# A hybrid decoder layer: the first adaLN sums in quarters of 256 channels, slots turned one pair ahead, one wait fewer before the router's sigmoid

## What is computed

```python
c_act = silu(c)
mod = c_act @ ada_w + ada_b                   # 1024 x 6144: shift, scale, gate of the mixer, then of the MoE
u = rms_norm(x) * norm_mix_g * (1 + scale_a) + shift_a
proj = u @ w_in                               # 1024 x 10760: q, k, v, o, gates of mLSTM; q, k, v of attention; g_m, g_a
y = sigmoid(g_m) * (mlstm(...) @ w_branch_m) + sigmoid(g_a) * (attention(...) @ w_branch_a)
x = x + gate_a * (y @ w_out)
v = rms_norm(x) * norm_ffn_g * (1 + scale_f) + shift_f
scores = sigmoid(v @ router_w)                # group-limited top 2 of 16 experts
x = x + gate_f * sum_e combine[e] * (silu(v @ w_gate[e]) * (v @ w_up[e])) @ w_down[e]
out = rms_norm(x) * final_norm_g
```

## Time and profile before

| what | value |
|---|---|
| median of three runs | 605.34 us |
| the profiled execution's own time | 606.29 us |
| span of its instructions | 604.5 us |
| TensorE busy | 581.9 us |
| VectorE busy | 307.1 us |
| ScalarE busy | 238.9 us |
| DMA | 184.78 MB, 306 GB/s over the span |
| granted TensorE clock, mean | 0.989 of full |

### The profile page before, as it was taken

One profiled execution on the slowest core, in us unless ns is written; L12 is line 12 of the kernel. 1 busy time (PEld: TensorE's weight loads), 2 busy tenths in 40 slices (PEclk: granted clock), 3 DMA queues, 4 the chain that ended last, 5 costly groups with the idle time before them and its releaser, 6 DMA issues.

```text
span 604.5 us, 8460 instructions
## 1 busy us (share of the span) xinstructions
PE 581.9 (96%) x3561; PEld 425.9 (70%) x3561; DVE 307.1 (51%) x461; ACT 238.9 (40%) x330; POOL 9.0 (1%) x23
## 2 busy tenths in 40 slices
PE   3999999999999999999999999899999999999995
PEld 1789988999998888999999988533533443353332
DVE  0679976766568876687455682602121130212204
ACT  4626647444455455674672334711111020111113
POOL 3010000000000000000000000000000000000000
PEclk9998999999999999999999999899999999999998
DMA  8999554785858946726659989299999999999991
GB/s 312 387 341 313 199 200 140 279 294 214 295 210 310 367 155 243 269 80 210 209 209 357 401 326 371 110 366 423 420 423 420 420 423 421 420 422 421 421 352 71
DMA packets 51578, 184.78 MB, mean 306 GB/s; under 512 B 3650, under 2 KB 3762, under 8 KB 37714
## 3 DMA queue, kind: packets, MB, share of 16 engines
q1 hardware_dynamic: 50706, 183.53, 78.8%
q10 hardware_dynamic: 704, 0.58, 0.3%
q0 software_dynamic: 128, 0.11, 0.1%
HBM read 183.16 MB, written 1.05 MB: 305 GB/s over the span
## 4 chain that ended last, share of the span: by engine, by line
PE 92%; ACT 3%; DVE 2%; DMA 1%; issue 1%; SPq 0%; ACTq 0%; DVEq 0%
PE ps L1571 30%; PE ps L1781 18%; PE ps L1593 15%; PE ps L1793 8%; PE ps L1827 3%; PE ps L1769 2%; DMA first_ada<-in_ada_w_dram 1%; PE ps L1552 1%; PE ps L1803 1%; PE ps L1657 1%; PE ps L1693 1%; PE ps L1678 1%; PE ps L1489 1%; PE ps L1820 1%; PE ps L1582 1%
## 5 line engine op out<-in xcount | busy, mean ns | idle before, releaser
L952 DVE TENSOR_TENSOR lo<-raw,hi 128x2048 fp32r<-128x2048 f32 (+1 forms) x51 | 114.2, 2248 | 42.1 <-ACT hi L612 41.8
L1571 PE MATMUL ps<-u_hi,hi 128*128 128x256 f32 x416 | 120.0, 288 | 0.4 <-DVE lo L952 0.4
L1571 PE MATMUL ps<-u_lo,hi 128*128 128x256 f32 x416 | 117.7, 283 | 0.0
L1571 PE MATMUL ps<-u_hi,lo 128*128 128x256 f32 x416 | 117.7, 283 | 0.0
L1781 PE MATMUL ps<-ring,xe_t 128*64 128x512 f32 x512 | 113.3, 594 | 0.0
L612 ACT CAST hi<-raw 128x2048 fp32r<-128x2048 f32 x50 | 94.8, 1908 | 37.2 <-PE ps L1571 26.3
L1781 PEld LDWEIGHTS ps<-ring,xe_t 128*64 128x64 f32 x512 | 35.9, 137 | 67.8 <-issue 67.4
L1571 PEld LDWEIGHTS ps<-u_hi,hi 128*128 128x128 f32 x416 | 79.7, 192 | 1.6 <-issue 0.8
L1571 PEld LDWEIGHTS ps<-u_lo,hi 128*128 128x128 f32 x416 | 79.7, 192 | 0.2
L1571 PEld LDWEIGHTS ps<-u_hi,lo 128*128 128x128 f32 x416 | 79.7, 192 | 0.0
L1793 PE MATMUL ps<-ring,he_t 128*64 128x512 f32 x224 | 49.6, 595 | 0.0
(11 more groups left out here) (332 smaller groups left out, 846.0 us busy)
## 6 DMA issues: line engine op xcount, KB each, us to landing
raw<-in_w_in_dram SPq DMA_DIRECT2D x41, 1024.0 KB, 5.4
ring<-in_w_gate_e_dram SPq DMA_DIRECT2D x32, 1024.0 KB, 17.2
ring<-in_w_up_e_dram SPq DMA_DIRECT2D x32, 1024.0 KB, 16.1
ring<-in_w_down_e_dram SPq DMA_DIRECT2D x28, 1024.0 KB, 16.0
raw<-in_ada_w_dram SPq DMA_DIRECT2D x16, 1024.0 KB, 5.3
first_ada<-in_ada_w_dram SPq DMA_DIRECT2D x16, 512.0 KB, 11.8
raw<-in_w_branch_m_dram SPq DMA_DIRECT2D x4, 1024.0 KB, 6.5
raw<-in_w_out_dram SPq DMA_DIRECT2D x4, 1024.0 KB, 5.6
```

The costliest lines, as they stand in the source:

```text
L952: ins = V.tensor_tensor(lo[b % RING][:, tiles, :], src[:, tiles, :], hi[b % RING][:, tiles, :].bitcast(F32), ALU.subtract)
L1571: ins = mm(dst, w[:, k, cols], x[:, k0 + k, :], start=(first and c % 2 == 0 and k == 0 and n == 0), stop=(end and k == KB - 1 and n == 2), ...
```

## The change

It has four parts.

1. The first six blocks are done as 12 pieces: four quarters of 256 channels by three groups of 512 columns. `first_ada` becomes two chunks of 1 MB for each quarter (four k by two vectors by 256 columns, in runs of 1 KB). For each quarter VectorE adds up the k in `SUMMED` into `acc_a`; TensorE multiplies the other k directly, with the weights as the stationary matrix and one column of c past it (`columns`), and adds `acc_a` by a column of ones. Row sums, the copy of rows and `pick_m` are gone. From the second quarter on ScalarE makes u_f32 too. Group 3 gets banks of its own. In the head x is turned in two parts, with the columns of quarter 0 between them, and 6 filler products wait for "vec".
2. Convolutions, gates, cumulative sum, mLSTM scores and values, and the scale after them stand up to two blocks later.
3. In the router one of two waits before the sigmoid is gone, a filler product stands in front of the wait for "picked", and the gather of the second part waits for "most" instead of "ranks", with `low_rows(1, 0)` in front of the ranks.
4. The slots of the next pair are turned behind `turn_he` of this pair, and VectorE takes them behind `weigh`. There are three scatter tiles instead of two. TensorE's wait before down is for the next pair's slots.

```diff
-BLOCKS = [(_g, _h * KB, _h == 0, _h == 1) for _h in range(2) for _g in range(EARLY)]
+QT = 2
+PIECES = [(_q, _g) for _q in range(KT // QT) for _g in range(EARLY)]
+FIRST_BLK = len(PIECES) // 2
+BLOCKS = [(0, 0, False, False)] * FIRST_BLK
...
-CONV_AT = {3: (0, 0), 4: (0, 1), 5: (1, 0), 6: (1, 1), 7: (2, 0), 8: (3, 0), 9: (3, 1), 10: (2, 1)}
+CONV_AT = {4: (0, 0), 5: (0, 1), 6: (1, 0), 7: (1, 1), 8: (3, 0), 9: (3, 1), 10: (2, 0), 11: (2, 1)}
-GATES_AT, CUMSUM_AT, GATE_T_AT, GATE_BACK_AT = 9, 11, 12, 13
-SCORE_M_AT = [14 + 2 * h for h in range(MH)]
-VALUE_M_AT = [15 + 2 * h for h in range(MH)]
-M_SCALE_AT = 22
+GATES_AT, CUMSUM_AT, GATE_T_AT, GATE_BACK_AT = 11, 13, 14, 15
+SCORE_M_AT = [16 + 2 * h for h in range(MH)]
+VALUE_M_AT = [17 + 2 * h for h in range(MH)]
+M_SCALE_AT = 24
...
-FIRST = ([("ada", a) for a in range(4)] + [("w", 0), ("w", 1), ("ada", 4), ("w", 2), ("ada", 5), ("ada", 6), ("ada", 7),
-                                           ("w", 3)])
+SUMMED = {0: (0, 1, 4, 5), 1: (0, 1, 2, 3, 4), 2: (0, 1, 2, 3, 4), 3: (0, 1, 2, 3, 4)}
...
-            n = g if g < EARLY else (g - EARLY) % 2
+            n = (1, 0, 2, 3)[g] if g <= EARLY else (g - EARLY) % 2
...
+            def load_ada(q):
+                for h in range(2):
+                    for m in range(2):
+                        sp.dma_start(first_ada[q][h][:, :, m, :], ada_first[:, KB * h:KB * (h + 1), m, q * T:(q + 1) * T]
+                                     ).then_inc(ada_landed[2 * q + h], 16)
...
+            for n, (q, g) in enumerate(PIECES):
+                if g == 0:
+                    if q == 2:
+                        after(sp, "x_ss", "x_t3")
+                    if q == 3:
+                        after(sp, "mod_col0")
+                    load_ada(q)
...
+                load_piece(n)
...
+            nc.gpsimd.memset(v_m[:, :, :, MD:MD + 1], 1.0).then_inc(ones_column, 1)
+            after(pool, "mod_col1")
             nc.gpsimd.memset(mod[:], 0.0).then_inc(acc_zero, 1)
...
+            x_up(0)
+            for n, (q, g) in enumerate(PIECES):
+                act.wait_ge(first_w[n], 16)
+                room(n)
+                if g:
+                    event(nc.scalar.copy(slab(hi, n), slab(raw, n)), f"hi{n}")
+                    if q == 0:
+                        for m in ((1,), (2, 3))[g - 1]:
+                            x_up(m)
+                    continue
+                for k in range(QT):
+                    event(nc.scalar.copy(slab(hi, n)[:, k, :], slab(raw, n)[:, k, :]), f"hi{n}_{k}")
+                after(act, f"chan{q}")
+                for k in range(QT):
...
+                    event(A_(u_hi[:, kk, :], x_t[:, kk, :], ACT.Identity, scale=chan[:, 2, kk:kk + 1], bias=chan[:, 0, kk:kk + 1]),
+                          f"u_hi{q}_{k}")
+                    if q:
+                        event(A_(u_f32[:, kk, :], x_t[:, kk, :], ACT.Identity, scale=chan[:, 2, kk:kk + 1],
+                                 bias=chan[:, 0, kk:kk + 1]), f"u_f32_{q}_{k}")
...
-            after(act, "logits_all0", "logits_all1")
+            after(act, "logits_all1")
             event(A_(rt[:, 0], rt[:, 1], ACT.Sigmoid), "scores")
...
+            def sum_ada(q):
+                acc = acc_a[:, q % 2].rearrange("p m n -> p (m n)")
...
+                for k in SUMMED[q]:
+                    dve.wait_ge(ada_landed[2 * q + k // KB], 32)
...
+                        ins = V.scalar_tensor_tensor(out=acc, in0=src, scalar=cs[:, k:k + 1], in1=acc, op0=ALU.mult, op1=ALU.add)
...
+            for n, (q, g) in enumerate(PIECES):
+                if g:
+                    after(dve, f"hi{n}")
+                    event(V.tensor_tensor(slab(lo, n), slab(raw, n), slab(hi, n).bitcast(F32), ALU.subtract), f"lo{n}")
+                    continue
+                sum_ada(q)
+                lo_tile(n, 0)
+                modulate(q)
...
-            V.tensor_reduce(many[:, 0:1], ps[5][:, TT * NE:(TT + 1) * NE], AX_X, ALU.max)
+            event(V.tensor_reduce(many[:, 0:1], ps[5][:, TT * NE:(TT + 1) * NE], AX_X, ALU.max), "most")
+            low_rows(1, 0).then_inc(xg_split, 1)
...
-                dve.wait_ge(slots_turned, p + 1)
-                take_slots(p % 2)
+                if p == 0:
+                    dve.wait_ge(slots_turned, 1)
+                    take_slots(0)
...
-                weigh(p % 2)
+                weigh(p % 3)
+                if p < PAIRS - 1:
+                    dve.wait_ge(slots_turned, p + 2)
+                    take_slots((p + 1) % 3)
...
+            def columns(q, k_of, begin, finish):
+                for k in k_of:
+                    pe.wait_ge(ada_landed[2 * q + k // KB], 32)
+                    for c in range(QT):
+                        for m in range(2):
+                            ins = mm(ps[column_bank(q)][:, 2 * c + m:2 * c + m + 1],
+                                     first_ada[q][k // KB][:, k % KB, m, c * P:(c + 1) * P], cs[:, k:k + 1],
...
+                if finish:
+                    after(pe, f"acc{q}")
+                    for c in range(QT):
+                        for m in range(2):
+                            ins = mm(ps[column_bank(q)][:, 2 * c + m:2 * c + m + 1], acc_a[:, q % 2, m, c * P:(c + 1) * P], ones[:, 0:1],
...
+            columns(0, left[0][0:2], True, False)
             pe.wait_ge(rows_loaded, 80)
             event(tr(ps[0][:, 0:96], rows[0:96, :], ident[0:96, 0:96]), "vec_t")
...
+            turn_x(0, range(KT))
+            columns(0, left[0][2:4], False, False)
+            turn_x(1, range(2))
+            columns(0, (), False, True)
+            turn_x(1, range(2, KT))
+            after(pe, "vec")
+            for n in range(6):
+                mm(ps[0][:, 0:P], ident[:], ones[:], start=True, stop=True)
...
+                    for c in range(4):
+                        if g == 2 and c == 2 and q < KT // QT - 1:
+                            columns(q + 1, left[q + 1], True, True)
+                        for k in range(QT):
+                            ins = products(c, k)
...
             start_sums(0, 0)
+            for _ in range(1):
+                mm(ps[3][:, 0:T], ident[:], mod[:, 0, 0:T], start=True, stop=True)
             after(pe, "picked")
...
-            after(pe, "ranks")
+            after(pe, "most")
             gather_part(1, 4 * SLOTS, 5, (0,))
...
-                pe.wait_ge(y_out, 2 * p)
                 if p == 0:
                     pe.wait_ge(weights_split, 1)
-                turn_slots(col, weights[:, :, 2 * p:2 * p + 2])
+                    turn_slots(0, weights[:, :, 0:2])
...
                 turn_he()
+                if p < PAIRS - 1:
+                    if p == 0:
+                        pe.wait_ge(scat_ready, 1)
+                    if p % 2:
+                        pe.wait_ge(onehot_ready, p // 2 + 2)
+                    turn_slots((p + 1) % 2 * 2 * SLOTS, weights[:, :, 2 * p + 2:2 * p + 4])
...
-                pe.wait_ge(scat_ready, p + 1)
+                pe.wait_ge(scat_ready, min(p + 2, PAIRS))
                 pe.wait_ge(he_t_ready, p + 1)
```

More of the change, by code:

```diff
@@ L668, in _, with x_up, room @@
-            split_first(0)
-            split_hi(1)
-            for s in range(NBLK):
-                if s + AHEAD < NBLK and s + AHEAD != EARLY and s != LAST_BLOCK[24]:
+                event(A_(x_in[:, t, :], x_in[:, t, :], ACT.Copy, scale=st[:, 6 + t:7 + t]), f"x_norm{t}")
+            def x_up(n):
+                after(act, f"x_t{n}")
+                event(nc.scalar.copy(x_t[:, 2 * n:2 * n + 2, :], ps[4 + n][:].rearrange("p (c t) -> p c t", c=2)), f"x_up{n}")
+            def room(n):
+                if n // 2 >= RING:
+                    act.wait_ge(block_done, n // 2 - RING + 1)
@@ L673, in _ @@
+            for s in range(FIRST_BLK - AHEAD, NBLK):
+                if s + AHEAD < NBLK and s != LAST_BLOCK[24]:
                     split_hi(s + AHEAD)
@@ new lines, in lo_tile, with modulate @@
+            def lo_tile(n, k):
+                after(dve, f"hi{n}_{k}")
+                event(V.tensor_tensor(slab(lo, n)[:, k, :], slab(raw, n)[:, k, :], slab(hi, n)[:, k, :].bitcast(F32), ALU.subtract),
+                      f"lo{n}_{k}")
+            def modulate(q):
+                after(dve, "vec", f"mod_col{q}")
+                half = slice(QT * q, QT * (q + 1))
+                step(V.tensor_tensor(chan[:, 0:2, half], ps[column_bank(q)][:, 0:2 * QT].rearrange("p (k a) -> p a k", a=2),
@@ L1031, in first_half, with u_tile @@
-            def first_half(j, row_bank, col_bank):
-                rows_out(j, row_bank)
-                lo_tile(j, 0)
-                modulate(j, col_bank)
-                for k in range(KB):
-                    if k:
-                        lo_tile(j, k)
-                    u_tile(j, k)
+                                             in1=vec[:, 64 + QT * q:64 + QT * (q + 1)], op0=ALU.add, op1=ALU.mult), f"chan{q}")
+            def u_tile(q, k):
+                kk = QT * q + k
+                if q == 0:
```

(24 more changed lines are left out.)

287 lines of the change are left out of this document (100 added, 187 removed).

## The result

The changed kernel is slower: median 615.61 us (614.03 to 617.96, 4 runs) against 605.67 us for the kernel before on the same chip (604.6 to 606.64, 4 runs), ratio 1.0167, 95% interval 1.014 to 1.0194. The forecast was 607.7 within 602.5 to 611.5: right in sign, too small in size, and the time lies outside the range. The four runs lie in two pairs, 614.03 and 614.05 us with a mean granted clock of 0.986, and 617.16 and 617.96 with 0.982 and 0.979; the profiled one is of the upper pair, so its trace holds 1.6 us more than the median.

The account below looks back on a forecast made before the run. TensorE, busy 96% of the span, was taken as the bound. Head +6.2, router -2.4 and expert loop -1.4 sum to +2.4 us: profiled execution 608.7, median 607.7, range with rivals 602.5 to 611.5.

Parts of the forecast that it names:

- The start: Head: first real product between 18.2 and 22.4 us, taken as 20.3, 2.3 us earlier than before.
- the bound of 22.4: Head: latest first product, with TensorE's small work at half clock, bounded at twice its time, 5.5 us.
- a landing at 12.65: Head: x and the first quarter's 2 MB of weights land at 12.15 us, plus 0.5 for 1 KB runs.
- The clock in the flow: Head, between quarters: half clock behind two of three column stages, 1.2 us each, 2.4 in all.
- The waits in the flow: Head, behind each quarter's columns: 2.2 us wait, 1.44 covered by half a piece, 0.8 left, 2.4 in all.
- Products and columns: Head: the 288 products stay 34.5 us; new small column products in three quarters take 3.4 each, 10.1 in all.
- VectorE's sums late: Rival, head: sums late at each quarter's closing columns, 3 x 1.2 us on top, 611.3 us; chance 0.08.
- The router: Router: earlier sigmoid table load gives 1.1 us, fuller clock lets 1.3 through, together 2.4 less (bounds 0 and 2.8).
- the filler should keep the clock: Router: shorter idling and the filler keep full clock at start_sums and gathers; 1.3 of 1.5 us comes through.
- The loop and the middle: Expert loop: slot turning moved, 1.4 us less (0 to 2.0); blocks moved by two: 0 (-0.5 to +1).
- The forecast's own bound for the head: Head: 6.2 us later expected, bounds +1.7 and +12.
- the unmoved load: Rival, router: the sigmoid's table load doesn't move, 1.1 us of gain lost, 608.8 us; chance 0.03.

Follow-up runs that it names:

- e9: e5 without the six filler products ahead of the first real product; 611.31 us, ratio 1.0098 to the kernel before.
- e10: e9 with all eight k of quarter 0 summed by VectorE; 609.0 us, ratio 1.0067 to the kernel before.
- e5: The changed kernel with the next quarter's column products spread over four places among the products of two pieces; 612.23 us, ratio 1.0121 to the kernel before.
- e3: The changed kernel with VectorE summing all eight k in quarters 1 to 3, TensorE keeping only closing columns; 613.05 us, ratio 1.0129 to the kernel before.
- e1: The kernel before with only parts 3 and 4 (router, slots); 601.25 us, ratio 0.9941 to the kernel before.
- e8: The kernel before with only one of the two waits before the router's sigmoid removed; 604.49 us, ratio 0.9974.
- e7: The kernel before with only the slots turned a pair ahead; 604.7 us, ratio 0.9979.
- e4: The changed kernel with 16 more filler products before the first columns; 616.14 us, ratio 1.0182 to the kernel before.

## Why the prediction was wrong

**The start was the step that failed most: 20.3 forecast, 24.48 measured.** Of the bounds, the late one was the truth. Closing columns end at 20.5 us, and u_lo is ready at 22.34, which is the bound of 22.4 almost to the tenth; I took the middle, on no row that showed one-column products at full clock so early. That the bound fits so closely is in part luck: it was built on a landing at 12.65, while the trace has TensorE start on the first columns at 9.80 and go through its list without a hole, never waiting for a landing again. The extra 0.5 us for runs of 1 KB is shown by no run either. The Trainium skill, "TensorE: Matmul & The Clock Gate", Part 4: PE-mode transpose, says that transposes don't count as busy for the clock as products do; the trace agrees: transposes took 1.71 / 8 = 0.21 us and one-column products 0.20 to 0.22, with TensorE never idle from 9.80 on. In the kernel before, behind row sums 512 columns wide, 16 such transposes took 0.12 each (chain of waits before):

```profile
14.13 1.97 PE ps L1510 x16
```

The other 2.1 us come from the fillers (12 x 0.21), which the sum left out: they wait for "vec", run at half clock too, and stand in front of the first product. By e9 they cost nothing to the end of the pieces, since without them the first products run at half clock in their place. The terms that I had given as causes for the late end were in part not needed: the DMA moved 346 to 357 GB/s at 9 to 12 us against 379 to 389 before, but TensorE, not the landing, was last (e10).

**The clock in the flow, the second step that failed.** I expected half clock behind two stages of three at 1.2 us; it came behind all three at 1.65, and e5, which spreads the same products and keeps 1.00, shows that their bunching brings it here. The first products at half clock, 0.7, were in no term.

**The waits in the flow.** 2.4 us forecast, none measured: the slow products covered them. Where the clock is full (e5) TensorE idles 0.57 a quarter. So waits and clock together were 4.8 in the sum and 5.6 in the trace; their split was wrong and their total nearly right.

**Products and columns.** 34.5 and 10.1 forecast, 34.6 and 10.4 measured: right. VectorE's sums late: not so in the changed kernel, right; the price of the rival was real, as e3 shows.

**The router.** The mechanism was right: -1.15 for the load, -2.15 in all in e1, against -1.1 and -2.4. What failed is the step "the filler should keep the clock", in the profiled execution: in it the half clock came 6 us earlier and lasted 6.8 us, over work (L1524, L1759, L1756) that the sum had at full clock or hidden beside VectorE. At half clock that list is the chain. It turned -2.15 into +0.4. Two of the four runs were 3.1 us faster than this one, so the step may have held in them; that isn't recorded. Even these, at 614.03 and 614.05, lie outside the range, by the head. On the drain of some 1.38 us that "ScalarE: Activation LUTs", What ACT_TABLE_LOAD costs, adds in the Trainium skill: e1 shows 0.02 us between load and sigmoid, and e8 gained 1.6 by its ratio (0.9 to 2.3), not 2.5; the measured row was the right choice.

**The loop and the middle.** -1.4 and 0, measured -1.4 and -0.1. e7 gives 1.3 by its ratio.

**The rest between forecast and result.** The profiled execution was to take 608.7 us and took 617.16: 5.3 more in the head, of which the start is 4.2, 2.8 more in the router, 0.4 in the tail. The forecast's own bound for the head reached +12, and the head came at +11.5; the range of the time, 611.5 at most, didn't carry that bound. The chances have a slip too: the unmoved load, at 608.8 and 3.5 over the median, belongs to slower, so same is 0.25 and slower 0.51.

## What to carry to other kernels

Here a run of one-column products, alone or with transposes, didn't keep TensorE's clock: price them at 0.21 us each, not 0.105, where no wide products stand in front, and charge the real products behind them as well. An edit that starts TensorE earlier has gained nothing until everything in front of the first real product is added up, fillers included. Before cutting finer, ask what each piece brings with it: here three stages of 3.5 us, in place of one of 2.6, were paid for a start that the forecast put at most 4.4 us earlier and the best variant (e10) got 2.9 earlier.

## What the runs showed of the hardware

- TensorE's clock was at half with TensorE busy for all of a stretch: 0.50 from 13 to 22 us in e4, and by the durations from 9.8 to 24 in the changed kernel. In that kernel's flow it fell from 1.00 to 0.50 at 36.3 us, behind 3.46 us of one-column products with no hole before or in them.
- The same small products spread among real ones went with a clock of 1.00 (e5), but made the real ones cost 0.129 us instead of 0.120.
- The DMA moved 346 to 357 GB/s between 6 and 12 us in the changed kernel (adaLN weights in runs of 1 KB), and 379 to 389 in the kernel before (runs of 2 KB).
- Executions with the same router code took from 13.7 to 16.4 us for it by where the half clock fell, and runs of one kernel differed by up to 4.1 us with the mean clock (e8: 602.97 at 0.999, 607.08 at 0.986).
